# Gate rows of two adaLN layers on VectorE instead of TensorE, and layer 1's shift and scale rows two passes sooner

## The reference, cut to what matters

```python
c_act = jax.nn.silu(c)                                            # 1 x 1024
for layer in range(2):
    ada = c_act @ w_ada[layer] + b_ada[layer]                     # w_ada[layer]: 1024 x 3072
    shift, scale, gate = jnp.split(ada, 3, axis=-1)
    h = rms_norm(x, norm_g[layer]) * (1.0 + scale) + shift        # wanted before the layer's projections
    y = (even_mixer, odd_mixer)[layer](h, ...)                    # projections, attention, output projection
    x = x + gate * y                                              # gate: wanted only at the layer's end
x = rms_norm(x, final_g)                                          # the second block follows
```

## Time and profile before

| | |
|---|---|
| median of 3 runs | 754.57 us (754.16 to 754.65) |
| the profiled execution, its time | 753.1 us |
| its span (first to last instruction) | 751.3 us |
| TensorE busy | 736.2 us, 98% |
| VectorE busy | 525.3 us, 70% |
| ScalarE busy | 380.7 us, 51% |
| GpSimd busy | 27.6 us, 4% |
| weights read | 144.68 MB, 194 GB/s over the span |

### The profile page before, as it was taken

How to read it: one execution, slowest core, us unless ns; L and a number is a source line. 1 busy time by engine, 2 the same in 40 slices (tenths; PEclk the granted TensorE clock), 3 DMA queues, 4 the chain that set the end, 5 groups by cost and what they waited for, 6 DMA issues and landing times.

```text
span 751.3 us, 11672 instructions
## 1 busy us (share of the span) xinstructions
PE 736.2 (98%) x4735; PEld 621.4 (83%) x4735; DVE 525.3 (70%) x729; ACT 380.7 (51%) x577; POOL 27.6 (4%) x43
## 2 busy tenths in 40 slices
PE   5999999999999999999999999999999999999998
PEld 2687886478888777788999999999988888888886
DVE  1486769648847867785789999747964868668431
ACT  2564567545354757555533454598443643534330
POOL 3000001001000000013000000000000000000000
PEclk9999999999999999999999999999999999999999
DMA  9994447924366363363745555423453653553711
GB/s 371 423 391 171 172 169 287 419 107 144 126 235 252 113 264 129 117 229 104 276 168 183 191 190 182 178 75 113 168 199 137 225 224 139 198 215 135 267 57 56
DMA packets 21956, 146.47 MB, mean 195 GB/s; under 512 B 2588, under 2 KB 2716, under 8 KB 5392
## 3 DMA queue, kind: packets, MB, share of 16 engines
q1 hardware_dynamic: 20880, 142.62, 50.8%
q0 software_dynamic: 752, 2.06, 0.9%
q10 hardware_dynamic: 272, 1.05, 0.4%
HBM read 144.68 MB, written 1.05 MB: 194 GB/s over the span
## 4 chain that ended last, share of the span: by engine, by line
PE 80%; DVE 3%; ACT 2%; issue 0%; POOL 0%; DVEq 0%; ACTq 0%
PE banks L465 19%; PE banks L467 18%; PE banks L466 18%; PE banks L544 8%; PE banks L545 5%; PE banks L575 3%; PE banks L664 1%; PE banks L599 1%; DVE WL L1720 1%; PE banks L546 1%; PE banks L707 1%; ACT WH L1202 0%; PE banks L631 0%; PE banks L951 0%; PE banks L936 0%; PE banks L711 0%
## 5 line engine op out<-in xcount | busy, mean ns | idle before, releaser
L1720 DVE TENSOR_TENSOR WL<-RAW,WH 128x2048 fp32r<-128x2048 f32 (+1 forms) x103 | 233.7, 2280 | 55.5 <-ACT WH L1202 55.0
L1202 ACT ACTIVATE WH<-RAW 128x2048 fp32r<-128x2048 f32 (+1 forms) x103 | 195.6, 1906 | 54.2 <-PE banks L467 41.0
L465 PE MATMUL banks<-HBOTH,WH 128*128 128x256 f32 x480 | 136.6, 285 | 0.0
L467 PE MATMUL banks<-HBOTH,WL 128*128 128x256 f32 x480 | 135.8, 283 | 0.0
L466 PE MATMUL banks<-HBOTH,WH 128*128 128x256 f32 x480 | 135.8, 283 | 0.0
L465 PE MATMUL banks<-WH,HBOTH 128*128 128x512 f32 (+1 forms) x320 | 127.4, 398 | 0.9 <-DVE HBOTH L2015 0.3
L467 PE MATMUL banks<-WH,HBOTH 128*128 128x512 f32 (+1 forms) x320 | 124.3, 388 | 0.0
L466 PE MATMUL banks<-WL,HBOTH 128*128 128x512 f32 (+1 forms) x320 | 124.1, 388 | 0.0
L465 PEld LDWEIGHTS banks<-HBOTH,WH 128*128 128x128 f32 x480 | 92.0, 192 | 1.1 <-issue 1.0
L466 PEld LDWEIGHTS banks<-HBOTH,WH 128*128 128x128 f32 x480 | 92.1, 192 | 0.1
L467 PEld LDWEIGHTS banks<-HBOTH,WL 128*128 128x128 f32 x480 | 92.0, 192 | 0.0
(11 more groups left out here) (303 smaller groups left out, 999.9 us busy)
## 6 DMA issues: line engine op xcount, KB each, us to landing
RAW<-in_weights_dram SPq DMA_DIRECT2D x114, 1024.0 KB, 4.8
BIG<-in_weights_dram SPq DMA_DIRECT2D x6, 1024.0 KB, 6.5
ROTS<-in_weights_dram SPq DMA_DIRECT2D x4, 1024.0 KB, 7.7
PROBS<-in_weights_dram SPq DMA_DIRECT2D x2, 1024.0 KB, 12.4
RAW<-in_weights_dram SPq DMA_DIRECT2D x2, 816.0 KB, 11.0
GATE<-in_weights_dram SPq DMA_DIRECT2D x3, 512.0 KB, 9.9
X<-in_x_dram ACTq DMA_DIRECT2D x1, 1024.0 KB, 5.6
QT<-in_weights_dram SPq DMA_DIRECT2D x1, 1024.0 KB, 13.3
```

The costliest lines, as they stand in the source:

```text
L465: pe.matmul(out_, lhsT=w[0], rhs=x[0], start=start, stop=False, **more)
L467: return pe.matmul(out_, lhsT=w[1], rhs=x[0], start=False, stop=stop, **more)
L1202: do(act.activation(WH[:, home[n], 0:kb * width], RAW[:, slot[n] % RAW_RING, 0:kb * width], ACT.Copy), high_done)
L1720: do(dve.tensor_tensor(WL[:, home[n], w], RAW[:, slot[n] % RAW_RING, w], WH[:, home[n], w], ALU.subtract), low_done)
```

## The change

The gate's rows leave TensorE. A new function on DVE multiplies each block of 128 x 512 with its column of CACT and adds it to ACC, whose row 0 holds the bias; the 128 partitions are then summed and spread by the same matmul as before, now with a matrix of ones. It is called in halves of four blocks and in parts of two: in layer 0 in passes 1, 2, 3, 7 and 8, for layer 1 ahead of its attention and in its passes 4 and 5. Layer 1's shift and scale rows move from TensorE's passes 7 to 10 to passes 5 to 8, in the order (1, 0), (1, 2), (1, 1), (1, 3). All their first halves have the home ROTS and all their second halves pair_rows. `gate_rows(0)` moves from pass 6 to pass 10, and ACT's `gate_out` behind it.

```diff
-    t += r4[:1] + za[1:] + zb + [out_[0][0]] + r4[1:] + [out_[0][1], out_[1][0]] + r5 + [out_[1][1]]
-    t += n0 + n1 + n2 + n3
+    t += r4[:1] + za[1:] + zb + r4[1:] + [out_[0][0]] + r5[:1] + n0[:1] + [out_[0][1]] + r5[1:] + [out_[1][0]] + n0[1:]
+    t += n2[:1] + [out_[1][1]] + n2[1:] + n1 + n3
...
-    t += rows("q1_0", "k1_0", "v1_0") + z1[:1] + rows("q1_1", "k1_1") + z1[1:2] + ada(1, 4) + last + z1[2:]
-    t += ada(1, 5) + list(out_[0]) + list(out_[1])
+    t += rows("q1_0", "k1_0", "v1_0") + z1[:1] + ada(1, 4) + rows("q1_1", "k1_1") + z1[1:2] + ada(1, 5) + last + z1[2:]
+    t += list(out_[0]) + list(out_[1])
...
+        idle, rots = [BIG[:, D:2 * D], GATE[:, :]], [ROTS[:, :]]
-                 ("ada0_4", 0, [pair_rows]), ("ada0_4", 1, [ROTS[:, :]]), ("ada0_5", 0, [pair_rows]),
-                 ("ada0_5", 1, [ROTS[:, :]]), ("ada1_1", 0, [pair_rows]), ("ada1_1", 1, [ROTS[:, :]]),
-                 ("ada1_3", 0, [pair_rows]), ("ada1_3", 1, [ROTS[:, :]]),
+                 ("ada0_4", 0, [pair_rows]), ("ada0_4", 1, idle), ("ada0_5", 0, [pair_rows]), ("ada0_5", 1, idle)]
+        areas += [(f"ada1_{c}", half, (rots, [pair_rows])[half]) for c in (0, 2, 1, 3) for half in range(2)]
...
+            (("ada0_5", 1), ("ada0_4", 1)), (("ada1_0", 1), ("ada0_5", 0)),
+            (("ada1_2", 0), ("ada1_0", 0)), (("ada1_2", 1), ("ada1_0", 1)), (("ada1_1", 0), ("ada1_2", 0)),
+            (("ada1_1", 1), ("ada1_2", 1)), (("ada1_3", 0), ("ada1_1", 0)), (("ada1_3", 1), ("ada1_1", 1)), ...
+        freed_by = {index[("ada0_4", 0)]: "kt.2", index[("ada0_4", 1)]: "hid.1", index[("ada1_0", 0)]: "qb.1.T"}
...  TensorE, layer 0
-                          5: [lambda: by_features("zb", 1), lambda: conditioning_row(0, 5), compressed_turn],
-                          6: [lambda: gate_rows(0)], 7: [lambda: conditioning_row(1, 0)], 8: [lambda: conditioning_row(1, 1)],
-                          9: [lambda: conditioning_row(1, 2)], 10: [lambda: conditioning_row(1, 3)],
+                          5: [lambda: by_features("zb", 1), lambda: conditioning_row(1, 0), compressed_turn],
+                          6: [lambda: conditioning_row(1, 2)], 7: [lambda: conditioning_row(1, 1)],
+                          8: [lambda: conditioning_row(1, 3)], 10: [lambda: gate_rows(0)],
-                      {4: [lambda: conditioning_row(0, 4)]}, {3: [compressed_scores]})
+                      last={3: [compressed_scores]})
...  TensorE, layer 1: conditioning_row(1, 4) leaves pass 4 and conditioning_row(1, 5) pass 7
...  ScalarE, layer 0, ahead of the exponentials of the pass
-                          }, {6: [gate_out]})
+                          }, {11: [gate_out]})
...  VectorE
+            def gate_row(layer, c, half, blocks=range(KB // 2)):
+                name = f"ada{layer}_{c}"
+                dve.wait_ge(gate_bias_in, 16 * (layer + 1))
+                dve.wait_ge(cact_ready, 1)
+                wait_raw(dve, name, half)
+                acc = ACC[:, c * 512:(c + 1) * 512]
+                for k in blocks:
+                    kk = half * KB // 2 + k
+                    do.after()
+                    do(dve.scalar_tensor_tensor(acc, raw_block(name, half, k), CACT[:, kk, 1:2], acc, ALU.mult, ALU.add),
+                       gate_read if k == KB // 2 - 1 else None)
...
+                          1: [lambda: gate_row(0, 4, 0), lambda: gate(0), lambda: rotate("qb", 1), lambda: lows(11)],
+                          2: [lambda: gate_row(0, 4, 1), lambda: gate_row(0, 5, 0, (0, 1)), lambda: lows(12)],
+                          3: [lambda: gate(1), lambda: gate_row(0, 5, 0, (2, 3)), compressed_mask],
+                          4: [lambda: lows(13), lambda: gate(2), compressed_probs, lambda: lows(14)],
+                          5: [lambda: lows(15)], 6: [lambda: lows(16), lambda: row_in(1, 0)],
+                          7: [lambda: gate(3), lambda: gate_row(0, 5, 1, (0, 1))],
+                          8: [lambda: gate_row(0, 5, 1, (2, 3)), lambda: row_in(1, 1)]})
...
+            lows(odd_first + 7)
+            gate_row(1, 4, 0)
+            lows(odd_first + 8)
+            gate_row(1, 4, 1)
             lows(odd_first + 9)
...
+                          4: [lambda: lows(odd_first + 15), lambda: gate_row(1, 5, 0)],
+                          5: [lambda: lows(odd_first + 16), lambda: gate_row(1, 5, 1)], 6: [lambda: lows(odd_first + 17), lambda: gate(2)],
+                          7: [lambda: lows(odd_first + 18), lambda: gate(3)],
```

More of the change, by code:

```diff
@@ L190, in two_blocks_kernel @@
         MS, RS = sb("MS", [P, 16, 8]), sb("RS", [P, 16, 8])
[L191 removed]
+        ONES, NM = sb("ONES", [P, P]), sb("NM", [P, n_units, 2])
         ES = sb("ES", [P, A_HEADS, 2])
@@ L296, in two_blocks_kernel @@
         raw_in = [sem(f"raw_in{r}") for r in range(RAW_RING)]
-        placed_in = [sem(f"placed_in{i}") for i in range(19)]
+        placed_in = [sem(f"placed_in{i}") for i in range(23)]
         high_done, low_done, piece_read = sem("high_done"), sem("low_done"), sem("piece_read")
@@ L409, in high_step @@
             return max(last_pair(layer, o) + 3, 7) if layer else max(last_pair(layer, o) + 3, 6 + o)
-        readers = {}
+        gate_pieces = [(f"ada{layer}_{c}", half) for layer in range(2) for c in (4, 5) for half in range(2)]
+        readers = {index[p]: (gate_read, n + 1) for n, p in enumerate(gate_pieces)}
         reads = [0]
@@ L590, in conditioning_half @@
             def conditioning_half(layer, c, half, kind="proj"):
-                row, name = (c // 2, f"ada{layer}_{c}") if c < 4 else (0, f"ada{layer}_{c}")
-                use = f"cols{layer}.{c % 2 if c < 4 else c}"
-                first, last = half == 0 and row == 0, half == 1 and (c >= 4 or row == 1)
+                row, name = c // 2, f"ada{layer}_{c}"
+                use = f"cols{layer}.{c % 2}"
+                first, last = half == 0 and row == 0, half == 1 and row == 1
                 bank = ps.open(pe, kind, use) if first else tiles[ps.uses[use][0]]
@@ L625, in gate_rows @@
             def gate_rows(layer):
-                for c in range(2):
-                    ps.wait_drained(pe, f"cols{layer}.{4 + c}")
-                pe.wait_ge(quads_set, 4)
+                pe.wait_ge(ones_set, 1)
+                pe.wait_ge(gate_read, 4 * (layer + 1))
                 for c in range(2):
                     bank = ps.open(pe, ("proj", "score")[layer], f"gate{layer}.{c}")
-                    mm = pe.matmul(bank[:, :], lhsT=QUADS[:, :], rhs=ACC[:, (4 + c) * 512:(5 + c) * 512],
+                    mm = pe.matmul(bank[:, :], lhsT=ONES[:, :], rhs=ACC[:, (4 + c) * 512:(5 + c) * 512],
                                    start=True, stop=True)
@@ L1120, in _, with shift_rows, gate_bias @@
         def _(pool):
-            def bias_rows(layer):
+            def shift_rows(layer):
+                pool.memset(ACC[:, 0:D], 0.0).then_inc(acc_clear, 1)
+                pool.wait_ge(acc_clear, 2 * layer + 1)
                 pool.dma_start(ACC[0:2, 0:D], bada_in[layer, 0:2 * D].rearrange("(r d) -> r d", r=2)).then_inc(bias_in, 16)
[L1123 to L1128, removed]
+            def gate_bias(layer):
+                pool.memset(ACC[:, 2 * D:3 * D], 0.0).then_inc(acc_clear, 1)
                 pool.wait_ge(acc_clear, 2 * layer + 2)
+                pool.dma_start(ACC[0:1, 2 * D:3 * D], bada_in[layer:layer + 1, 2 * D:3 * D]).then_inc(gate_bias_in, 16)
             pool.dma_start(CST[:, 0:P], consts_in[:, 0:P]).then_inc(ident_in, 16)
[L1132 to L1138, removed]
+            shift_rows(0)
+            gate_bias(0)
+            pool.memset(ONES[:, :], 1.0).then_inc(ones_set, 1)
             pool.memset(HALFNEG[:, :], -0.5).then_inc(consts_set, 1)
@@ L1762, in row_in @@
                 bank = ps.wait_filled(dve, use)
-                dve.wait_ge(bias_in, 32 * (layer + 1))
+                dve.wait_ge(bias_in, 16 * (layer + 1))
                 acc = ACC[:, c * 512:(c + 1) * 512]
                 ps.drain(dve.tensor_tensor(acc, acc, bank[:, :], ALU.add), use)
+            def gate_row(layer, c, half, blocks=range(KB // 2)):
[9 more added lines that the diff above has]
+                       gate_read if k == KB // 2 - 1 else None)
             def modulation(layer, use, blocks):
@@ L2087, in _ @@
                               lambda: rotate("qb", 0), lambda: lows(10)],
-                          1: [lambda: gate(0), lambda: rotate("qb", 1), lambda: lows(11)], 2: [lambda: lows(12)],
-                          3: [lambda: gate(1), compressed_mask],
-                          4: [lambda: lows(13), lambda: gate(2), lambda: row_in(0, 4), compressed_probs, lambda: lows(14)],
-                          5: [lambda: row_in(0, 5), lambda: lows(15)], 6: [lambda: lows(16)], 7: [lambda: gate(3)],
-                          9: [lambda: row_in(1, 0)], 10: [lambda: row_in(1, 1)]})
+                          1: [lambda: gate_row(0, 4, 0), lambda: gate(0), lambda: rotate("qb", 1), lambda: lows(11)],
```

(7 more changed lines are left out.)

15 lines of the change are left out of this document (8 added, 7 removed), and 3 rows, old and new, of the table follows.

## The result

The changed kernel takes 765.26 us (median of 4 runs, 763.62 to 765.58) against 754.37 us (4 runs, 753.42 to 754.65): ratio 1.0145, 95% interval 1.0128 to 1.0162, or 10.9 us more where 3.4 more were forecast. The profiled execution has a span of 763.8 us (765.58 with what lies around it), 12.5 more than before's. The two traces stand further apart than the medians: the changed kernel's is of its slowest run (mean granted clock 0.986; the other three had 0.991), before's is of a run at 1.000.

The account below looks back on a forecast made before the run. TensorE, busy for 98% of the span, was taken to bound the kernel. Layer 0 loses 6.4 us and layer 1 gains 3.0: +3.4 on the median of 754.57 gives 758.0 us, range 754.5 to 761.5.

Parts of the forecast that it names:

- The clock: Rival: after pass 6's 4 us wait TensorE runs slower for a while, costing 1.5 us: 759.5 us; chance 0.17.
- the median stands 1.5 above the profiled execution: Sum: +3.4 on the profiled 753.1 gives 756.5; the runs' median stands 1.5 higher, so 758.0 us.
- The loads: Layer 0, passes 5 to 8: two homes refilled only after each reading; late landings make pair 9's scores 6.5 us late.
- Passes 4 and 9: Layer 0: each loses a row set, but the exponentials limit the pass; gains of 0.41 and 0.38 us, not 1.85.
- VectorE's blocks: Gate rows as 32 dependent operations 0.73 us apart; six take 4.4 into pass 2's pause of 4.48; cost zero.
- `gate_out`: Layer 0, pass 11: it now comes after the copies, so TensorE waits 0.4 us for the bank.
- Layer 1: Two row sets go, 3.7 us, of which 0.7 becomes a wait for the heads' low parts: 3.0 us gained.
- the rival of a late VectorE: Rival: room in pass 2 and layer 1's passes 4 and 5 fails, layer 1's 3.0 lost: 761 us; chance 0.07.
- Loads in time: Rival: layer 1's row loads arrive when wanted, so the change gains 3.8 us: 750.8 us; chance 0.15.
- Waits at half: Rival: the load waits come out at about half, near 754.6 us, no change; chance 0.08.

Follow-up runs that it names:

- layer 1 only: The kernel before with the gate's rows on VectorE for layer 1 only, layer 0 and its loads untouched: 752.47 us, ratio 0.9978.
- fillers everywhere: The changed kernel with thrown-away transposes in TensorE's long waits of passes 4, 6, 8 and 9: 763.64 us, ratio 1.0127 against the kernel before.
- one piece earlier: The changed kernel with wo0_1's second half issued ahead of both halves of ada1_2: 759.85 us, ratio 1.0068 against the kernel before.
- no reloads: The changed kernel with six pieces (ada1_2, ada1_1, ada1_3) not loaded, their rows computed from ada1_0's data: 753.44 us, ratio 0.9989 against the kernel before.
- filler in pass 4: The changed kernel with 14 thrown-away transposes in pass 4's wait for the probabilities: 765.71 us, ratio 1.0151 against the kernel before.

## Why the prediction was wrong

The direction, the place and the mechanism of the loads were as forecast. The size was 7.5 us short in layer 0 and 0.4 in layer 1 (11.3 of engines' work for 3.4). These numbers compare two traces, and the medians are 10.9 apart.

**The clock: the step that failed.** The forecast's sum has no term for it. It stood among the rivals, with the right place, 1.5 us and a chance of 0.17. In the changed kernel's trace it fell at three places, and along the path that ended last it takes 5.7 us. In pass 4 and the projection behind it, pair 4's scores to pair 5's took 5.52 (4.81 with the filler), from there to the row set 8.26 (7.04 with fillers), 1.9 in all. Pass 6: the reading at the lower clock delays the next issue by 0.9 (2.00 from its start to the issue, for 1.10 to 1.12 elsewhere). Behind pass 8: 2.7, and 0.2 into pass 9. Of the 1.9 us that pass 6 lost to the clock, only those 0.9 reached the next landing, since the rest fell into the time for it. The rival priced the wait of 4 us at about a third of what it bounded it by (4.4), and neither it nor the forecast had a price for the waits of pass 8 or for pass 4.

Pass 4's fall is only in part the change's. It comes in "layer 1 only" as well, with layer 0 untouched, and about half of the kernel before's runs have a fall somewhere. The forecast had seen that the median stands 1.5 above the profiled execution, and added it without asking what it was.

**The loads: right in this trace, but not independent of the clock.** A home that is read in four passes running is refilled only after each reading, and the landing takes 4.7 for the first and 8.8 for the third of three (forecast 4.8 and 8.9, by the 2.5 a piece of the earlier trace rows). Waits of 6.9 for 7.5. The two later landings took 0.3 and 0.55 more than forecast (5.1 for 4.8, 6.3 for 5.75). That they agree so well is in part luck: with the clock held full ("fillers everywhere") the landings took 10.0, 4.7 and 7.7, and the last reading of the home in BIG came 38.7 us after pair 4's scores (110.26 to 148.92), for 39.4 in the changed kernel and 35.3 in the forecast (109.57 to 144.9). So of the 5.7 us only the 2.9 behind the last landing are the clock's alone. The 2.8 ahead of it come out of this trace's path, and where the falls were held off, longer landings took the place of all but 0.7 of them; without any fall ahead of that reading the forecast would still have been 3.3 us short there. That the order of one piece mattered was in the forecast's timeline, but not that it was worth 5.4 us.

**Passes 4 and 9: a limit mis-read.** The forecast named the exponentials as the limit of a pass and gave 0.41 and 0.38. The limit is VectorE's chain: scores, peaks, normalising of the pair before, turn, scores, 4.75 us (148.34 to 153.09 in "one piece earlier"), against the 4.76 that pass 9 had with its row. TensorE's wait there is 1.82, ended by line 1928. The rows had filled these waits almost exactly, so that before showed none, and the gain was 0.1 at most in pass 4 and none in pass 9: 0.7 us more of the miss.

**The rest of layer 0.** VectorE's blocks ran 0.79 apart and not 0.73, and six of them take 4.7 where the pause had 4.48; pair 4's scores came 0.15 late (109.72 for 109.57). VectorE's timeline:

```profile
85.97 3.12 DVE L1778 SCALAR_TENSOR_TENSOR BIG<-BIG,CACT 128x512 f32<-128x512 f32 x4
```

The sum up to layer 1: 6.4 (forecast) + 5.7 (clock) + 0.7 (passes 4 and 9) + 0.85 (the two later landings) + 0.15 = 13.8, for 13.9 measured. `gate_out` cost a wait of 0.19 for the 0.4 forecast, but from pair 10's scores to layer 1 the path lost 0.3, as forecast.

**Layer 1.** -1.88 and -1.85 for the two row sets, and a wait for the low parts of the heads, with the chain around it 1.1 and not 0.7. Its visible part, TensorE's timeline:

```profile
311.32 0.47 PE L468 MATMUL banks<-WH,HBOTH 128*128 128x512 f32 x1 [0.90 <-DVE HBOTH L1953]
```

-2.6 for -3.0. VectorE hid everything else there, so the rival of a late VectorE fell.

**The rivals.** Loads in time is refuted by the waits, and "no reloads" shows what it would have given: not the 3.8 us of the forecast but some 2.5, since layer 0 has nothing to give in passes 4 and 9. Waits at half didn't occur.

Shown by runs: the cost of the late loads (no reloads), of the one piece's place, of layer 1, the worthlessness of pass 4's row, and that clock and loads overlap (filler in pass 4, fillers everywhere). Only read from traces, one of each kernel: the split of the 13.9 and the 2.7 behind pass 8. Open: what makes the clock fall in pass 4 in some runs and not in others, and why the landings took longer when TensorE asked for them sooner.

## What to carry to other kernels

Count a home's round trip before its traffic: reading, issue, landing, and compare it with the work between two readings; a home that is refilled between neighbouring passes paces the loop at that trip, and then neither a faster TensorE nor a held clock helps. Before a matmul is counted as a gain, ask which chain of the other engines the pass would hit without it; here it had filled exactly the wait that took its place. And price a new wait of some microseconds on TensorE twice, once for the wait and once for matmuls at half speed behind it, except where the next wait swallows them; here it came behind 3.91 and 5.23 us, and not behind the 1.35 and 1.95 of "one piece earlier". Where a median stands above the profiled run, ask what the other runs had before adding the difference.

## What the runs showed of the hardware

The granted clock fell in pass 4 while TensorE had no wait above 0.3 us behind it: the four matmuls at 111.22 took 1.12 instead of 0.65, and in a kernel with the gate's row set still there the same four took 1.08. With 14 transposes in the pass's wait the clock stayed full there in two profiles; in a third it fell ahead of them. One kernel's runs differ by such falls: 753.2, 755.0 and 756.7 us on average at mean clocks of 1.000, 0.998 and 0.995 for the kernel before, some 1.7 us each. After a wait of 3.91 us the scores at 139.44 were at full speed again (0.93), after one of 5.23 us the same scores at 140.19 weren't (1.65). Waits of 1.1 and 1.4 us close together were followed by the lower clock in one kernel and not in another. Three pieces of 1 MB issued within 0.9 us landed 4.7, 6.9 and 8.8 us after their issues (418 GB/s from 130 to 135 us); in the two kernels with filler in pass 4 and these loads the third took 10.0 and 10.2.
